# Four runs of 1, 2, 3 and 3 tiles instead of three of 2, 3 and 4, and ranking one group ahead instead of two

## The reference, cut to what matters

```
h = rmsnorm(x);  z = h @ w_in                      # 1024 x 2720
branches: latent attention, differential attention, memory attention   # causal in chunks of 64
merged = sum over branches of sigmoid(h @ w_gate_b) * (o_b @ w_br_b)
x = x + merged @ w_o
h2 = rmsnorm(x);  q = h2 @ peer_wq;  sc = q @ subkeys        # 8 heads x 2 x 128 scores
per token and head: top 16 of each half, top 16 of their 256 sums -> idx (16), g = softmax
a = gelu(peer_u[idx] . h2);   y = sum over heads and k of g * a * peer_v[idx]
out = rmsnorm(x + y)
```

## Time and profile before

| | |
|---|---|
| median of three runs | 4415.14 us (4411.97 to 4420.18) |
| profiled execution, own time | 4452.41 us |
| its span, first to last instruction | 4450.6 us |
| busy: PE, DVE, POOL, ACT | 64%, 55%, 53%, 18% |
| moved by the DMA queues | 1388.83 MB, 312 GB/s over the span |
| mean granted TensorE clock | 0.76 |

### The profile page before, as it was taken

The page is one execution under the profiler, slowest core; times in us unless marked ns, Lnnn a source line. Parts: engine busy times, 40 slices in busy tenths (PEclk is TensorE's granted clock), DMA queues, the critical chain, the costliest instruction groups (busy, mean ns, idle before and its releaser), DMA issues.

```text
span 4450.6 us, 39027 instructions
## 1 busy us (share of the span) xinstructions
PE 2849.2 (64%) x12071; PEld 1499.1 (34%) x12071; DVE 2446.5 (55%) x6358; ACT 795.1 (18%) x1696; POOL 2346.7 (53%) x2128
## 2 busy tenths in 40 slices
PE   7779668777897878677777799783233233233334
PEld 5468546434453434443434344341000000000000
DVE  1241454677344456387788455566665666666651
ACT  1230012333111112133333111111000000000000
POOL 0000224344343346376666564567777777777774
PEclk9769889777998989877777899896555555656556
DMA  7244668777977979899999998899999999999998
GB/s 243 89 140 137 227 233 309 252 257 263 330 274 267 341 274 397 284 331 355 339 337 330 362 373 322 319 376 363 363 375 366 379 371 378 368 370 364 371 367 284
DMA packets 552141, 1388.83 MB, mean 312 GB/s; under 512 B 51296, under 2 KB 253024, under 8 KB 551936
## 3 DMA queue, kind: packets, MB, share of 16 engines
q0 software_dynamic: 304128, 1107.43, 67.0%
q1 hardware_dynamic: 227408, 249.27, 17.1%
q10 hardware_dynamic: 20400, 29.64, 2.0%
HBM read 1326.10 MB, written 60.05 MB: 311 GB/s over the span
## 4 chain that ended last, share of the span: by engine, by line
PE 34%; POOL 23%; issue 13%; DVE 12%; DMA 10%; ACT 4%; DVEq 2%; another core or an unknown queue 1%; SPq 1%; ACTq 0%; POOLq 0%
POOL G_v_rows L569 12%; POOL G_u_rows L569 11%; PE scores L695 8%; PE scores L1452 8%; PE y_sum L1942 4%; PE scores L1456 4%; PE scores L1641 3%; DVE G_u_rows L1778 3%; DMA G_v_rows<-in_peer_v,G_idxT 2%; PE scores L1538 2%; DMA DF_w_br<-scratch_skT 2%; ACT C_probs L1260 2%; DVE C_probs L1327 1%; PE o L1209 1%; DVE C_probs L1351 1%
## 5 line engine op out<-in xcount | busy, mean ns | idle before, releaser
L569 POOL DMA_INDIRECT G_v_rows<-in_peer_v,G_idxT x1056 | 1180.9, 1118 | 1066.6 <-PE y_sum L1942 720.9
L1778 DVE CUSTOM_DVE_ANT_0 G_u_rows<-G_u_rows,G_h 128x1024 f32<-128x1024 f32 x1056 | 1276.3, 1221 | 529.5 <-DMA G_u_rows<-in_peer_u,G_idx 482.5
L569 POOL DMA_INDIRECT G_u_rows<-in_peer_u,G_idx x1056 | 1161.6, 1100 | 726.7 <-issue 314.4
L1942 PE MATMUL y_sum<-G_v_rows,G_zw 128*32 128x512 f32 x4224 | 792.5, 888 | 1000.9 <-DMA G_v_rows<-in_peer_v,G_idxT 961.8
L1942 PEld LDWEIGHTS y_sum<-G_v_rows,G_zw 128*32 128x32 f32 x4224 | 155.7, 142 | 1531.5 <-issue 1526.2
L1452 PE MATMUL scores<-D_hT,D_w_gate 128*128 128x256 f32 (+2 forms) x768 | 238.2, 464 | 0.0
L695 PE MATMUL scores<-A_w_in,A_hT 128*128 128x256 f32 (+2 forms) x864 | 223.5, 420 | 9.7 <-ACT A_hT L783 5.6
L695 PEld LDWEIGHTS scores<-A_w_in,A_hT 128*128 128x128 f32 x864 | 171.1, 200 | 63.3 <-issue 14.3
L1192 PE MATMUL turn<-ident,C_probs 128*128 128x128 f32 (+1 forms) x647 | 142.1, 337 | 72.1 <-ACT C_pT L1272 52.5
L1452 PEld LDWEIGHTS scores<-D_hT,D_w_gate 128*128 128x128 f32 x768 | 145.2, 191 | 92.7 <-issue 54.2
L548 POOL MEMSET G_zw<- 128x1024 f32 x2 | 1.8, 956 | 292.8 <-SPq L521 292.8
(11 more groups left out here) (282 smaller groups left out, 3822.0 us busy)
## 6 DMA issues: line engine op xcount, KB each, us to landing
A_w_in<-in_w_in SPq DMA_DIRECT2D x24, 1024.0 KB
D_w_gate<-in_w_gate SPq DMA_DIRECT2D x24, 1024.0 KB
G_u_rows<-in_peer_u,G_idx POOLq DMA_INDIRECT x1056
G_v_rows<-in_peer_v,G_idxT POOLq DMA_INDIRECT x1056
DF_w<-in_w_gate SPq DMA_DIRECT2D x12, 1024.0 KB
DF_w<-in_peer_wq SPq DMA_DIRECT2D x12, 1024.0 KB
F_w_q<-in_peer_wq SPq DMA_DIRECT2D x12, 1024.0 KB
G_sc<-scratch_sc ACTq DMA_DIRECT2D x66, 128.0 KB
```

Of the source, the lines that this page charges most:

```text
L569: pool.indirect_dma_start(out=buf[:, :], out_offset=None, in_=table, in_offset=bass.IndirectOffsetOnAxis(ap=rows, axis=0)).then_inc(signal ...
L1778: dve.tensor_tensor_reduce(out=self.u_rows[slot][:, :], in0=self.u_rows[slot][:, :], in1=self.h2[t % 2][:, :], scale=1.0, scalar=0.0, op0= ...
L1942: last = pe.matmul(self.ps_y[32 * c:32 * (c + 1), cols], self.zw[b % 2][:, at:at + 32], self.v_rows[(4 * quad + c) % SLOTS_G][:, cols], st ...
```

## The change

The spans become tiles 0; 1 and 2; 3 to 5; 6 to 8. `AHEAD` goes from 2 to 1: a group is ranked during the group just before it, in the steps 0, 2, 4 and 6 of it rather than 3, 6, 9 and 12, with its gate in step 8 rather than 15; only one group is ranked ahead of the first step. The end of a span's dense work moves from 48 steps ahead of its first tile to 24 (the 2 and the `AHEAD` in the two formulas are the ticks of the first ranks). With the new list the first span ends at step 21, the second at 105 (`inputs` to 37, `attend` to 67, `merge` to 87), the third at 361 (150, 258, 313), the fourth at 745 (434, 613, 680). The loads of scores and of `h2` come later by as much. Three places allow for a span of one tile: a probability buffer of at least 256 columns, no second load of x, and the last head pair's norm after the last job.

```diff
-SPANS = [Span(i, lo, hi) for i, (lo, hi) in enumerate(((0, 2), (2, 5), (5, TILES)))]
+SPANS = [Span(i, lo, hi) for i, (lo, hi) in enumerate(((0, 1), (1, 3), (3, 6), (6, TILES)))]
-AHEAD = 2
+AHEAD = 1
-        top = sp.keys
+        top = max(sp.keys, MEM)
...
-                out += [0] * 5 + [1, 2] + [2 + 3 * k for k in range(1, 2 * HEADS - 6)]
+                out += [0] * 5 + [1] + [1 + 2 * k for k in range(1, 2 * HEADS - 5)]
...
-            end = 2 + P * sp.tiles[0] - (AHEAD + 1) * TOPK
+            end = AHEAD + P * sp.tiles[0] - 24
...
-        self.load_x(eng, sp, 1)
+        if sp.nt > 1:
+            self.load_x(eng, sp, 1)
...
         take_o(len(jobs) - 1)
+        if o.last["diff"] + 2 == o.n:
+            norm_o(PAIRS - 1)
...
-                if c in (3, 6, 9, 12):
-                    self.rank(dve, m, c // 3 - 1)
-                if c == 15:
+                if c in (0, 2, 4, 6):
+                    self.rank(dve, m, c // 2)
+                if c == 8:
                     self.gate(dve, m)
...
         self.load_scores(act, 0)
+        self.load_h2(act, 0)
         self.load_scores(act, 1)
-        self.load_h2(act, 0)
         self.gate_exp(act, 0)
-        self.load_scores(act, 2)
-        yield
-        self.gate_exp(act, 1)
         yield
...
-            if c == 8 and n + 3 < GROUPS_ALL:
-                self.load_scores(act, n + 3)
-            if c == 10 and n + AHEAD < GROUPS_ALL:
+            if c == 8 and n + AHEAD + 1 < GROUPS_ALL:
+                self.load_scores(act, n + AHEAD + 1)
+            if c == 5 and n + AHEAD < GROUPS_ALL:
                 self.gate_exp(act, n + AHEAD)
...
-            if n % HEADS == 4 and c == 5 and t + 1 < TILES:
+            if n % HEADS == 6 and c == 12 and t + 1 < TILES:
                 self.load_h2(act, t + 1)
```

More of the change, by code:

```diff
@@ L501, in weave @@
             done += 1
-        assert done == STEPS + 2, done
+        assert done == STEPS + AHEAD, done
     def dense(self, inputs, memory, attend, merge, out, score, eng):
@@ L1521, in out_sp @@
         self.load_score(eng, sp, 0)
-        for k in range(2):
+        for k in range(min(2, nt)):
             eng.wait_ge(self.e_out[k], self.e_out0[k][i] + 32 * ((nt + 1 - k) // 2))
@@ L1968, in _ @@
         def _(sp):
-            k.weave(k.dense(k.inputs_sp, k.memory_sp, k.attend_sp, k.merge_sp, k.out_sp, k.score_sp, sp), idle(sp, STEPS + 2))
+            k.weave(k.dense(k.inputs_sp, k.memory_sp, k.attend_sp, k.merge_sp, k.out_sp, k.score_sp, sp), idle(sp, STEPS + AHEAD))
         @block.tensor
```

## The result

The changed kernel takes 4453.66 us (median of four runs, 4453.4 to 4456.19), the kernel before 4417.66 on the same chip: ratio 1.0084, 95% interval 1.0067 to 1.0102. It is 36 us slower. A second set of runs gave 1.0092 (1.0069 to 1.0115), 4497 against 4458 us. The profile of before that the prediction used (4450.6 us) lies some 35 us above the timed runs beside it; the profile after (4451.5 us) belongs to a set in which the kernel before took 4418. That the two spans are equal says nothing.

A forecast was written before the change was run, and what follows sets the result against it. Dense work bounds the first span, transfers the end; 418 + 588 + 1095 + 1395 + 996 = 4492 us against 4451, 41 us more. Put on the median of the timed runs, the forecast was 4457 us, range 4335 to 4545.

The forecast's parts named there:

- What bounds it: Whole kernel: dense work sets the first span's time, transfer bounds the end at share 0.97 and 363 GB/s.
- Queue work: Whole kernel: 51.5 MB more, 157 us of added transfer time on 3836, and 520 us of idle, making 4513 us.
- First span: One tile instead of two: 418 us against 577, bounds 390 and 500, with `attend` at 80 us.
- waits for keys: Rival, `attend` of the first two spans: three reloads stalling 10 us each, for two kinds, add 60 to 80 us; chance 0.12.
- cold TensorE: Rival, first span: 128-column work at 1.2 GHz makes the span 500 us and the whole kernel 4574 us; chance 0.08.
- Second span: Two tiles with 84 steps: 588 us, bounds 540 and 650.
- a step's price of 1.8 us: Expert steps under dense work: VectorE's 1.78 us a step, taken as 1.8 for each step that isn't hidden.
- `out` with `score`: Second span: 103 us of dense work and 18 steps, 135 us.
- The late rank "costed at nothing": Expert steps: ranking later costs nothing, as the rank stays two steps ahead of the gather that needs it.
- Elastic cover: Rival, second and third spans at the queues' pace, 560 and 1000 us: total 4369 us, in the median 4334; chance 0.25.
- Full cover: Rival, whole kernel: the dense stream ends at 3019 as before and 435 us fall away, 4015 us; chance 0.03.
- the third span's upper bound: Third span: at most 1171 us, with 74 more steps at the full 2.89 us.

The follow-up runs named there:

- again: The changed kernel measured once more, unaltered, against the kernel before: ratio 1.0092 (1.0069 to 1.0115).
- copies in the fourth span: Changed kernel, each fourth-span load of w_in, w_gate and peer_wq also copied to unused HBM (32 MB): ratio to the kernel before 1.0279, 84 us over the changed kernel.
- 24 steps more: Old three spans with the new rank, dense work ending 24 instead of 48 steps ahead: ratios to the kernel before 0.9879 against 1.0064.
- the four spans with the early rank: Kernel before with the changed spans, still ranking two groups ahead and dense work ending 48 steps ahead: ratio to the kernel before 1.0154 (1.014 to 1.0168).
- the control: The kernel before, unchanged, against itself: ratio 1.0005 (0.9991 to 1.0019), medians 4453 and 4449 us, profile 4440.8.
- 8 and 16 steps more with the early rank: Kernel before, dense work ending 40 or 32 steps ahead instead of 48 (32 also loads scores later): ratios to the kernel before 0.993 and 0.9926.
- the fourth load with its later end: Changed kernel with spans of 2, 2, 2 and 3 tiles: ratio to the kernel before 1.0013 (0.999 to 1.0036).

## Why the prediction was right

**The forecast,** 41 us more than before, was met by 36 and 39 (ratio 1.0093 by the sum of stages, 1.0084 and 1.0092 measured). Most of the agreement is earned by the stages. Part of it is luck: the first span was forecast 17 to 23 us too long and the second 24 to 34 too short, and these cancel.

| us | forecast | profile after | again |
|---|---|---|---|
| first gather | 368 | 348.5 | |
| first span | 418 | 394.8 | 400.5 |
| second | 588 | 622.2 | 611.9 |
| third | 1095 | 1084.0 | 1100.0 |
| fourth | 1395 | 1358.0 | 1386.8 |
| the end | 996 | 992.0 | 1001.8 |
| sum | 4492 | 4451 | 4501 |

The last column is the fair one, since in its set the kernel before took 4458 us.

**What bounds it** was right: the fourth span and the end run at 0.97 to 0.98, and copies in the fourth span cost their full price. Queue work plus 136 us where I had 157, idle 480 where I had 520.

**First span.** `inputs` and `memory` together 148.5 (forecast 147), `merge` 75 (80), to the first gather 60.7 (61), the rest of `score` 46 (50). Mis-sized: `attend`, 64 where I had 80. It took 3.2 us a job, against 2.87 with two tiles. The waits for keys that the rival named did come, but small: TensorE waited for the reloads three times, 8.5 us in all, and in the second span for none but the first, 5.8 us. The rival wanted 10 us for each of the three in both spans, and fell. The cold TensorE fell too: the clock was 0.95 in `merge` at 128 columns, though 0.50, its lower level (1.2 GHz), through all of `attend`, where it was busy 37 of 64 us. The rule of the Trainium skill (TensorE: Matmul & The Clock Gate, "HAM oscillation — how this bites in real kernels") fits `attend` in part: of TensorE's waits there 20 us were for loads and 14 for VectorE and ScalarE. In `merge` the waits for loads that it needs did not come, but for 9.5 us, most of them at its start.

**Second span,** the term that was mis-sized: 588 us, measured 622 and 612. Two things are in it.

The first is a step's price of 1.8 us. The runs put it at 0.2 (24 steps more for 4.3 us) to 1.0 (31 steps fewer: 580.7 us in the four spans with the early rank, 611.9 in the changed kernel again); beside the control, 8 and 16 steps more with the early rank lengthen the second span by 10 us each. That VectorE's time for a step mostly fits into its waits for other engines is the likely reading, and was not measured. With 1.8 taken off for each of 180 steps I made the dense work of the earlier trace rows too cheap; `inputs` came to 138 for 130, `attend` to 183 for 178.

The second, and the larger, is `out` with `score`: 156 for 135. A cheaper step would have made this forecast smaller, not larger. I had 103 us for its dense work, taken from a chain in which the weights of `score` were there in time; in the new second span the chain waited 57 us for them, at a share of the queues of 0.66. The whole span stood at a share of 0.70 to 0.71, as forecast. The third and the fourth span, at shares of 0.91 and 0.98 mostly held by their transfers, came within 11 and 37 us.

**The late rank "costed at nothing"** was wrong. No wait for an index appeared in the changed kernel but the first, 134.0 us, as I said:

```profile
  DVE G_idx L1742: 134.0, 1
```

Yet at the old deadline it costs 0.64%. Beside the control, from another set, that kernel is 7 us longer in the second span (which has 8 steps more), 28 in the third (1498.8 against 1470.7) and 18 at the end (1452.4 against 1434.9). These 53 us are more than the 29 of the ratio, and with the deadline at 24 the same late rank has 1473.9 in the third span, so they don't say where the loss sits; the cause stays open. The run also has one rank less ahead of the first step, and the first span's end at step 21 rather than 29, which were not tried apart. What is shown is that the rank's place matters: with its last piece six steps later in the group it cost 2.1% more.

**The rivals.** Elastic cover, the one that ends faster, needed the third span under 1045 us; it took 1084 and 1100 at a share of 0.91 and 0.90. Full cover fell as argued: the dense stream ended at 3459 and not at 3019.

**The sum as a story** holds with other weights: the new deadline gives 82 us, the late rank takes 29 back, the fourth load with its later end costs 55, and the single first tile 35. Each is the step from one tested version to the next, so that they add up to the whole is no proof, and in another order they can come out otherwise. I had the first tile as the gain (159 us less ahead of the second span) and the load as the loss; but what the first span saved, the second gave back, with only 84 steps in it.

Two slips in the working change nothing: the third span's upper bound counts 74 steps more where 256 less 180 are 76, and the cold TensorE's losses of 69, 15 and 20 us make 104 and not the 82 of its 500.

Not tried: a first span of one tile with spans of four and four, without a fourth load.

## What to carry to other kernels

When a deadline-bound stream (dense work that must be done before step N) is woven with a transfer-bound one, book each stretch as queue work and idle, and move steps only out of full stretches into idle ones; starting the transfer-bound stream earlier was worth nothing here, where its steps were then missing under the next stretch. A low share of the queues doesn't mean that loads come in time: ask which load the chain waits for. Cutting the deadline's slack was the cheap gain, 2 to 4 us a step, as long as the rank's pieces came early enough, and another pass over the weights was not. Test a change of two parts in its parts: here one was worth 1.0 to 1.2% and the other cost 1.9 to 2.1%.

## What I had not expected of the hardware

The same program's median moved by 1.3% from set to set (4418 to 4475 us); the rate of the full queues varies too, 353 to 366 GB/s over the end of the profiles. For the changed kernel both moved together (361 GB/s beside a control of 4418 us, 357 beside 4458); but the first profile of before has 363 at 4451 us, so the rate alone doesn't give the level. A copy of 32 MB within HBM costs 84 us in a full stretch, 2.6 us a MB, less than the 3.05 that SyncE's queue shows by its share of the engines, and 44 us in a stretch whose queues idle 29% of the time. And in a one-tile `attend`, TensorE busy 57% of the time, the granted clock was at its lower level throughout.
